# Reordering the modulation sums, two weight loads and one weight split around the end of the first block's attention mixing

## The reference

```python
mod = silu(c) @ w_mod + b_mod              # 6 x 1024: sh_m, sc_m, gt_m, sh_f, sc_f, gt_f
...
merged = sigmoid(gate_a) * (o_a @ w_br_dsa) + sigmoid(gate_b) * (o_b @ w_br_moba)
x = x + gt_m * (merged @ w_out)
h = rms_norm(x, g_ffn_norm) * (1.0 + sc_f) + sh_f
g_ff, u_ff = split(h @ w_gate_up)
x = x + gt_f * ((silu(g_ff) * u_ff) @ w_down)
```

## Time and profile before

| quantity | value |
|---|---|
| profiled execution, its own time | 1496.65 us |
| span from first to last instruction | 1494.3 us |
| mean granted TensorE clock | 0.992 |
| TensorE (PE) busy | 1444.0 us, 97% |
| VectorE (DVE) busy | 848.9 us, 57% |
| ScalarE (ACT) busy | 689.7 us, 46% |
| DMA moved | 271.13 MB, mean 181 GB/s |

### The profile page before, as it was taken

One profiled execution on the slowest core, in us unless ns is written; L12 is line 12 of the kernel. 1 busy time (PEld: TensorE's weight loads), 2 busy tenths in 40 slices (PEclk: granted clock), 3 DMA queues, 4 the chain that ended last, 5 costly groups with the idle time before them and its releaser, 6 DMA issues.

```text
span 1494.3 us, 17957 instructions
## 1 busy us (share of the span) xinstructions
PE 1444.0 (97%) x6902; PEld 1155.1 (77%) x6902; DVE 848.9 (57%) x1029; ACT 689.7 (46%) x875; POOL 36.2 (2%) x53
## 2 busy tenths in 40 slices
PE   6999999999999999999999999999999988999998
PEld 3657777688888888888888888778888865788887
DVE  2686865654556545466755445565545667655444
ACT  2554453544344443444453444754344676554442
POOL 0010100000000000000000000200000020000000
PEclk8999999999999999999999999999999999999999
DMA  9853766455564655646555655565565620355651
GB/s 344 287 207 117 250 212 238 157 196 186 180 196 157 209 179 186 196 157 202 177 182 184 196 176 191 148 196 178 189 194 175 193 92 1 113 178 189 190 190 71
DMA packets 188164, 271.13 MB, mean 181 GB/s; under 512 B 8381, under 2 KB 134149, under 8 KB 188101
## 3 DMA queue, kind: packets, MB, share of 16 engines
q1 hardware_dynamic: 186448, 267.01, 54.5%
q10 hardware_dynamic: 1492, 2.98, 0.6%
q0 software_dynamic: 160, 0.26, 0.2%
HBM read 269.19 MB, written 1.05 MB: 181 GB/s over the span
## 4 chain that ended last, share of the span: by engine, by line
PE 85%; DVE 6%; ACT 3%; DMA 3%; issue 2%; SPq 1%; POOL 0%; ACTq 0%; DVEq 0%
PE bank L1799 26%; PE bank L1801 25%; PE bank L1800 25%; DVE w_lo_ring L1309 2%; PE bank L1829 2%; ACT w_hi_ring L964 1%; PE bank L1969 1%; DMA arena<-in_w_mod_dram 1%; DMA raw_ring<-in_w_in_dram 1%; PE bank L1937 1%; DMA raw_ring<-in_w_out_dram 1%; PE bank L2120 1%; PE bank L2023 1%; DMA raw_ring<-in_nsa_w_qg_dram 0%; SPq L867 0%
## 5 line engine op out<-in xcount | busy, mean ns | idle before, releaser
L1309 DVE TENSOR_TENSOR w_lo_ring<-raw_ring,w_hi_ring 128x2048 fp32r<-128x2048 f32 (+1 forms) x228 | 518.3, 2277 | 414.0 <-ACT w_hi_ring L1252 329.5
L1799 PE MATMUL bank<-w_hi_ring,h_hi 128*128 128x512 f32 x1360 | 543.4, 400 | 3.0 <-DVE h_lo L1453 1.1
L1801 PE MATMUL bank<-w_hi_ring,h_lo 128*128 128x512 f32 x1360 | 531.4, 391 | 0.0
L1800 PE MATMUL bank<-w_lo_ring,h_hi 128*128 128x512 f32 x1360 | 530.6, 390 | 0.0
L1252 ACT ACTIVATE w_hi_ring<-raw_ring 128x2048 fp32r<-128x2048 f32 x158 | 302.6, 1915 | 295.5 <-PE bank L1801 292.2
L1799 PEld LDWEIGHTS bank<-w_hi_ring,h_hi 128*128 128x128 f32 x1360 | 255.9, 188 | 68.1 <-issue 15.1
L1801 PEld LDWEIGHTS bank<-w_hi_ring,h_lo 128*128 128x128 f32 x1360 | 255.7, 188 | 55.0
L1800 PEld LDWEIGHTS bank<-w_lo_ring,h_hi 128*128 128x128 f32 x1360 | 256.3, 188 | 49.5
L1799 PE MATMUL bank<-w_hi_ring,f_hi 128*128 128x512 f32 (+1 forms) x456 | 177.0, 388 | 0.0
L1801 PE MATMUL bank<-w_hi_ring,f_lo 128*128 128x512 f32 (+1 forms) x456 | 175.9, 386 | 0.0
L1800 PE MATMUL bank<-w_lo_ring,f_hi 128*128 128x512 f32 (+1 forms) x456 | 175.7, 385 | 0.0
(11 more groups left out here) (257 smaller groups left out, 851.3 us busy)
## 6 DMA issues: line engine op xcount, KB each, us to landing
raw_ring<-in_ffn_w_gate_up_dram SPq DMA_DIRECT2D x176, 512.0 KB
raw_ring<-in_ffn_w_down_dram SPq DMA_DIRECT2D x44, 1024.0 KB
raw_ring<-in_w_in_dram SPq DMA_DIRECT2D x22, 1024.0 KB
raw_ring<-in_w_gate_up_dram SPq DMA_DIRECT2D x44, 512.0 KB
arena<-in_w_mod_dram SPq DMA_DIRECT2D x18, 1024.0 KB, 7.5
raw_ring<-in_w_down_dram SPq DMA_DIRECT2D x11, 1024.0 KB
raw_ring<-in_conv_w_in_dram SPq DMA_DIRECT2D x16, 512.0 KB
raw_ring<-in_w_mod_dram SPq DMA_DIRECT2D x6, 1024.0 KB
```

Of the source, the lines that this page charges most:

```text
L1309: dve.tensor_tensor(w_lo[:, u % RING, 0:words], raw[:, r % RING, 0:words], w_hi[:, u % RING, 0:words].bitcast(F32), ALU.subtract).then_inc ...
L1799: pe.matmul(dst, hi, whi, start=start, stop=False)
L1800: pe.matmul(dst, hi, wlo, start=False, stop=False)
L1801: return pe.matmul(dst, lo, whi, start=False, stop=stop)
```

## The change

The plan's items are reordered in one stretch; no operation of the computation is added or dropped, and the three matmuls of `hold` are removed.

```diff
-    part("bb", 1, 0, 1, [mod_row2(9), evac("ba", 0), mod_sum(9), evac("bb", 1), tgroup("merged", 4)[:2]])
-    add("mod_a", norm=1, half=0)
-    by_token_tile("ba", 1, 0, 1, behind=mod_load(10))
-    part("out1", 0, 0, 2, [mod_load(11)], [tgroup("merged", 4)[2:], []])
+    part("bb", 1, 0, 1, [mod_row2(9), evac("ba", 0), evac("bb", 1), tgroup("merged", 4)[:2]])
+    by_token_tile("ba", 1, 0, 1, last=True)
+    part("out1", 0, 0, 2, [], [tgroup("merged", 4)[2:] + [dict(kind="then split", unit=len(units) - 1)], []])
+    plan.extend(mod_load(10))
     part("out1", 0, 1, 2, [evac("out1", 0)])
+    plan.extend(mod_load(11))
     part("out1", 1, 0, 2)
     by_token_tile("out1", 1, 1, 2, last=True)
     add("square")
     add("scale_x", norm=1)
-    plan.extend(mod_row2(10) + mod_row2(11) + mod_sum(10) + mod_sum(11))
-    plan.extend(tgroup("normf", 4, norm=1)[:2] + hold(3, 4))
-    begin_glu("f0", 1, FIRST_PAIR[0], tgroup("normf", 4, norm=1)[2:])
+    plan.extend(mod_sum(9) + mod_row2(10) + mod_row2(11))
+    add("mod_a", norm=1, half=0)
+    plan.extend(tgroup("normf", 4, norm=1)[:2] + mod_sum(10))
+    begin_glu("f0", 1, FIRST_PAIR[0], tgroup("normf", 4, norm=1)[2:] + mod_sum(11))
```

## The result

The changed kernel takes 1501.01 us (median of 18 runs, 1499.29 to 1504.45), the kernel before in the same series 1497.05 (18 runs, 1495.23 to 1501.72). The ratio is 1.0026, with a 95% interval of 1.0019 to 1.0033. That is slower by 4 us, beyond the stated range (to 1500.7); the forecast was 1498.1.

What follows compares the result with a forecast made beforehand. TensorE, holding 85% of the chain of waits, was taken as the bound. From 1496.65 us, 1.0 gained at full clock and 2.7 lost to the low clock gave 1498.35, less 0.28: 1498.1, range 1494.3 to 1500.7.

Steps and rivals of the forecast that it cites:

- A shift there is taken as a shift of the end: At the start of `gu` sub 1 (283.98 before): any shift there moves the kernel's end equally.
- the start value: Time of before that the shift was added to: profiled execution 1496.65 us, median of runs 0.28 below it.
- the full-clock sum: Net at `gu` sub 1 if the clock stays up: 283.0 against 283.98, 1.0 us gained.
- the clock: Low clock on the second `mod_row2` (+1.82) and the sum of piece 10 (+0.87): 2.7 us lost, bounds nothing and 6.2.
- Part 1: Up to the last `out1` unit: earlier `merged` transposes and waits removed, 2.9 us gained.
- Part 2: x updates: the last ends at 266.7 instead of 272.06, 5.4 us earlier.
- Part 3: Norm's wait to `gu` sub 1: moved sums wait for banks, spending most of x's gain; `gu` sub 1 at 283.0.
- Rival C: Clock still low at first feed-forward products because `hold` is gone: 1500.5 to 1501.6 us; chance 0.21.
- Rival A: Clock stays up through the changed stretch: about 1495.4 us; chance 0.12.
- milder form: Only `mod_row2(11)` runs at the low clock: 1497.2 us; chance 0.2.
- Rival D: Tail costs nothing, sums find banks free and x's 5.4 us arrive whole: 1491.1 us; chance 0.09.

Runs made afterwards that it cites:

- before_delay: Kernel before with five unread matmuls (2.1 us) added behind `gu` sub 1; 2.9 us above the median of its own runs of before.
- loads_only: Kernel before with only the loads of pieces 10 and 11 moved to their new places; 1494.94 us.
- hold_back: Changed kernel with the three idle `hold` matmuls put back behind `normf` 1, ahead of the sum of piece 10; median 1.7 us higher than the changed kernel's.
- changed: The changed kernel itself, in its first profiled execution of 1503.68 us; median of its 18 runs 1501.01 us.
- after_again: The changed kernel unchanged, run for a second trace; stage 61.0 us and attention 219.1 us again.
- after_delay: Changed kernel with three unread matmuls (1.3 us) added behind `gu` sub 1; median 0.7 us below the changed kernel's.
- sum11_behind: Changed kernel with the sum of piece 11 behind `gu` sub 1 instead of ahead of it; median 4.9 us lower than the changed kernel's.
- old_tail: Kernel before with only the change's first half (up to the last `out1` unit), its tail as before with `hold`; 1491.20 us.
- sum9_ahead: Changed kernel with the sum of piece 9 moved between `square` and `scale_x`; median 2.2 us shorter than the changed kernel's.
- new_tail: Changed kernel with loads and split as before, sum of piece 9 still in the new tail; 1505.63 us.
- old_tail_no_hold: Kernel before with the change's first half and the tail as before, but without the three `hold` matmuls; 1492.79 us.

## Why the prediction was wrong

- **The step that failed** is "A shift there is taken as a shift of the end", with its ground, that TensorE "runs on without waiting" behind `gu` sub 1. The start of `gu` sub 1 was forecast at 283.98 + 1.7 = 285.7; it came at 285.99 in a trace whose times are 0.29 late, so at 285.70, or at 286.0 if counted by the second matmul. The stage was right within 0.3. The trace of before has only 3.0 us of TensorE waits from there to 1101 us, but 12.1 us in the sparse attention, up to 2.0 us long, with a PEclk of 0.97 over 100 us; the row at 1216 lies in it. Some 900 us behind the change this stage ran 4.7 us longer in the profiled pair, by the clock and not by its waits. All fourteen traces have the middle the same within 0.2 us, and an attention between 213.5 and 219.3.
- By the medians the forecast, 1498.1, was 2.9 us too low. Of these, 0.7 is the start value (three runs of before gave 1496.37, eighteen gave 1497.05). The other 2.3 are the shift: 4.0 where 1.7 was forecast, 0.3 of it in the stage. The remaining 2 us lie outside the stage if before usually runs as it was profiled; if it often keeps the full clock in the stage, as in `before_delay`, up to 1 of them is a longer loss in the stage.
- That the stage came out so near is partly luck: the full-clock sum was 0.3 us too high (a gain of 1.3 and not 1.0), the clock 0.6 too low, as below.
- Part 1 was right: 1.35 us forecast at `merged` 0; 1.04 measured, and 1.33 counted from the start of `mod_row2(9)`. The 1.06 us wait and the fourth unit's went. The largest single cause is the order of the loads, by `loads_only`.
- Part 2 was right: the last update of x at 266.7 against 266.83, or 266.54 without the late start.
- Part 3 was right in each wait: 2.7 forecast and 2.79 measured for the second `mod_row2`, "about 1.8" and 1.53 for piece 10, "about 2" and 1.86 for piece 11.
- The clock was forecast at 2.7 us, 1.8 on the second `mod_row2` and 0.9 on the sum of piece 10. Measured are 1.7 (3.60 against 1.92), 0.7 up to the second matmul of `gu` sub 0 (1.89 us behind the start of the sum, against 1.19 in `hold_back`, where the clock was full), and 0.9 on the rest of `gu` sub 0 (3.45 against 2.54 there), which the forecast had left out: 3.3 together. It fell twice, with full clock between, and did not stay low beyond `gu` sub 0, as the forecast had said. Its sentence that the same kernel can meet the clock otherwise from run to run is borne out by the three traces of before's code.
- Rival C was nearest in time (1500.5 to 1501.6) for a partly wrong reason. It blamed the missing `hold`, which `hold_back` speaks against; the slow `gu` sub 0 it named was there, but the stage lost 2.0 us and not the 3.9 to 5.2 of C, so that its time fits is chance. (C's 1500.5 leaves out the 0.28 us that its other end, 1501.6, subtracts; it should be 1500.2.) Rival A fell, in its milder form too: in five traces with the hole of 2.79 us ahead of the second `mod_row2` (`changed`, `after_again`, `after_delay`, `hold_back`, `sum11_behind`) the clock was at 0.50 within a microsecond of it, and in the four of them without `hold` again under `gu` sub 0. By the rule of the Trainium skill on idle gaps ("TensorE: Matmul & The Clock Gate", section "Why this matters for your kernels") gaps of this size would not have cost the clock; here the measurement decides against it. Rival D, a tail that costs nothing, is not this change but is what the old tail delivers behind the new first half.
- The range ended at 1500.7 because it held no term for later stages, and none for how far the runs of before lie apart.

What stays open: what decides how much of the attention runs at the lower clock, and why `sum11_behind` and `old_tail` come off better there than `sum9_ahead`, `loads_only` or `new_tail`. Within one kernel the runs spread by up to 6.5 us (before: 1495.23 to 1501.72), so each kernel may well meet short and long forms, and only one or two traces per kernel show which.

## What to carry to other kernels

An operation put into a wait is only hidden if its eviction does not queue behind the thing being waited for: here a 0.15 us VectorE operation behind `scale_x` held a bank, and with it 1.9 us of matmuls and everything behind them. When filling a wait, follow the buffer of each moved item to who frees it and to what stands ahead of that in the freeing engine's queue. And compare kernels by stage, since a stage that nobody touched can move the total by more than the edit does; and take a second trace of the kernel before, since its own stage can differ by 1 us from run to run.

## What the runs showed of the hardware

- Small holes can cost the clock, and the same hole in the same code does not always. After 2.79 us idle (five traces of the changed kernel and its variants) the granted clock was 0.50 each time; in the profiled one 16 records of `mod_row2` took 3.60 us and not 1.92. After 2.18 to 2.23 us (three traces of before's code) it was 0.50 soon in one, 0.50 a microsecond later in the second, and 1.00 throughout in the third: 3.58, 2.82 and 1.95 us for the same two sums.
- Shorter holes went both ways too. After 1.53 us (ahead of the sum of piece 10, changed kernel), with the 2.79 us hole 5 us earlier, it was 0.50; after 1.53 us in `old_tail_no_hold`, with TensorE at work without a longer gap for 7 us ahead, it stayed 1.00. The same 1.86 us wait ahead of the sum of piece 11 was followed by 1.00 in the changed kernel and by 0.50 in `hold_back`.
- With three dummy matmuls in such a hole (one trace) the low stretch lay on `gu` sub 1 and not on `gu` sub 0, and the stage was 61.0 us as without them.
- One and the same attention stage takes 213.5 to 219.3 us, with a PEclk of 0.98 to 0.90 over 100 us and no more waiting of TensorE in the long form than in the short; in one pair of traces a delay of 1.3 us, 900 us ahead of it, went with 4.6 us less in it.
